# Norm roots on ScalarE, their inverses and the rotary turn on VectorE, GpSimd left with the gathers

## What is computed

```
def rms_norm(x, g):
    y = xf * rsqrt(mean(xf * xf, axis=-1) + EPS)
    return y * g

layer:
    h = modulate(rms_norm(x, norm1), shift, scale)            # 1024 wide
    z = h @ w_in                                              # q, k, v | pool | cq, ckv, krope
    q_na, k_na = rms_norm(q_na), rms_norm(k_na)               # per head of 64
    q_mla = rms_norm(rms_norm(cq) @ w_uq)                     # per head of 96
    ckv = rms_norm(ckv);  k_mla = rms_norm([ckv @ w_ukv, krope])
    sample tokens: the last 32 of each head of q_mla and k_mla get an axial rotary turn
    three mixers (windowed attention, pooling, latent attention) -> x = x + g1 * (mix @ w_out)
    h2 = modulate(rms_norm(x, norm2), shift, scale)
    experts: 8 heads x 16 experts of 16384 per token; u row . h2 -> gelu -> sum of weighted v rows
    x = x + g2 * experts
```

## Time and profile before

| | us |
|---|---|
| median of 3 runs | 4089.07 (4085.47 to 4100.49) |
| the profiled execution's own time | 4087.34 |
| its span, first to last instruction | 4084.9 |
| PE busy | 3017.2 (74%) |
| DVE busy | 2633.4 (64%) |
| POOL busy | 2578.4 (63%) |
| ACT busy | 365.9 (9%) |
| moved over the span | 1504.70 MB, 1342.34 MB of them by the gathers |

### The profile page before, as it was taken

The page is one execution under the profiler, slowest core; times in us unless marked ns, Lnnn a source line. Parts: engine busy times, 40 slices in busy tenths (PEclk is TensorE's granted clock), DMA queues, the critical chain, the costliest instruction groups (busy, mean ns, idle before and its releaser), DMA issues.

```text
span 4084.9 us, 36679 instructions
## 1 busy us (share of the span) xinstructions
PE 3017.2 (74%) x10978; PEld 1092.4 (27%) x10978; DVE 2633.4 (64%) x7013; ACT 365.9 (9%) x1055; POOL 2578.4 (63%) x2836
## 2 busy tenths in 40 slices
PE   7888988778766666777767888877777766666666
PEld 4534443223222122322211335332322301011000
DVE  2555568768665665667667555776776767666663
ACT  2112111101000010101000111110100000000000
POOL 1157357667575666766667654656776777777775
PEclk8999799878787677877866997888887967676667
DMA  7887999999999999999999997999999999999998
GB/s 280 307 299 281 325 378 406 390 396 397 360 373 389 399 366 342 348 341 409 387 408 406 332 338 264 349 373 379 398 384 354 395 409 408 404 405 403 400 409 343
DMA packets 453356, 1504.70 MB, mean 368 GB/s; under 512 B 47108, under 2 KB 67368, under 8 KB 452648
## 3 DMA queue, kind: packets, MB, share of 16 engines
q0 software_dynamic: 368640, 1342.34, 84.9%
q1 hardware_dynamic: 84108, 159.92, 10.8%
q10 hardware_dynamic: 412, 0.11, 0.0%
HBM read 1496.52 MB, written 5.67 MB: 368 GB/s over the span
## 4 chain that ended last, share of the span: by engine, by line
DMA 35%; PE 28%; POOL 19%; issue 12%; DVE 5%; ACT 1%; SPq 0%; ACTq 0%; DVEq 0%; POOLq 0%
DMA expert_rows<-in_peer_v,pair_experts 28%; POOL expert_rows L1105 18%; PE expert_sum L2267 11%; DMA expert_rows<-in_peer_u,experts 5%; PE work L1993 4%; PE work L2193 3%; PE work L2208 2%; DVE expert_rows L1903 2%; PE work L2129 2%; PE work L1939 1%; PE work L2156 1%; PE work L1968 1%; POOL stat_rstd L1055 1%; PE work L2174 1%; DMA weight_ring<-in_w_mod 1%
## 5 line engine op out<-in xcount | busy, mean ns | idle before, releaser
L2267 PE MATMUL expert_sum<-expert_rows,weight_columns 128*32 128x512 f32 x5120 | 1704.5, 767 | 849.8 <-DMA expert_rows<-in_peer_v,pair_experts 839.5
L1903 DVE CUSTOM_DVE_ANT_0 expert_rows<-expert_rows,tokens 128x1024 f32<-128x1024 f32 x1280 | 1558.8, 1218 | 865.1 <-DMA expert_rows<-in_peer_u,experts 856.3
L1105 POOL DMA_INDIRECT expert_rows<-in_peer_v,pair_experts x1280 | 1228.1, 959 | 780.1 <-PE expert_sum L2267 526.3
L1105 POOL DMA_INDIRECT expert_rows<-in_peer_u,experts x1280 | 1214.7, 949 | 475.4 <-issue 346.5
L2267 PEld LDWEIGHTS expert_sum<-expert_rows,weight_columns 128*32 128x32 f32 x5120 | 213.4, 119 | 1794.4 <-DMA expert_rows<-in_peer_v,pair_experts 1550.8
L1993 PE MATMUL work<-weight_ring,h_or_mixed 128*128 128x384 f32 (+3 forms) x768 | 258.3, 494 | 15.4 <-DMA weight_ring<-in_w_in 8.4
L1939 PE MATMUL work<-ident,scratch 128*128 128x128 f32 (+1 forms) x770 | 153.7, 327 | 119.3 <-DVE scratch L1501 41.9
L1993 PEld LDWEIGHTS work<-weight_ring,h_or_mixed 128*128 128x128 f32 x768 | 146.8, 207 | 145.2 <-issue 86.7
L2208 PE MATMUL work<-h_or_mixed,weight_ring 128*128 128x128 f32 (+1 forms) x1024 | 166.2, 320 | 8.5 <-DMA weight_ring<-in_peer_wq 3.5
L1939 PEld LDWEIGHTS work<-ident,scratch 128*128 128x128 f32 (+1 forms) x770 | 101.3, 161 | 264.6 <-issue 118.2
L2208 PEld LDWEIGHTS work<-h_or_mixed,weight_ring 128*128 128x128 f32 x1024 | 145.7, 203 | 64.5 <-issue 57.2
(11 more groups left out here) (210 smaller groups left out, 2706.2 us busy)
## 6 DMA issues: line engine op xcount, KB each, us to landing
weight_ring<-in_w_mod SPq DMA_DIRECT2D x20, 2048.0 KB, 14.7
expert_rows<-in_peer_u,experts POOLq DMA_INDIRECT x1280, 7.7
expert_rows<-in_peer_v,pair_experts POOLq DMA_INDIRECT x1280, 7.6
weight_ring<-in_w_in SPq DMA_DIRECT2D x11, 1536.0 KB, 14.9
weight_ring<-in_peer_wq SPq DMA_DIRECT2D x8, 2048.0 KB, 12.6
weight_ring<-in_w_out SPq DMA_DIRECT2D x7, 2048.0 KB, 19.1
mla_qkv_or_x_and_queries<-in_w_out SPq DMA_DIRECT2D x8, 1280.0 KB, 6.3
expert_rows<-in_w_mod SPq DMA_DIRECT2D x4, 2048.0 KB, 14.1
```

The source lines that it names most:

```text
L1105: g.indirect_dma_start(buffer, None, table, bass.IndirectOffsetOnAxis(ap=numbers[:, col:col + 1], axis=0),).then_inc(row_in, 16)
L1903: v_.tensor_tensor_reduce(out=u_ring[r % U_RING], in0=u_ring[r % U_RING], in1=tokens[:, :], scale=1.0, scalar=0.0, op0=ALU.mult, op1=ALU.a ...
L2267: ins = t_.matmul(acc[to:to + STRIP_T, hf * 512:(hf + 1) * 512], spread[:, at:at + STRIP_T], v_buffer(row)[:, hf * 512:(hf + 1) * 512], st ...
```

## The change

POOL no longer takes part in norms or in the rotary turn; after the setup its stream holds gathers alone.

- ACT's squares are scaled by n**-0.5 where the mean was wanted (`mean_scale`), so sums become means; for A and uq they stay sums, as before.
- ACT does a new step `root` right behind each of its squares: `stat_std` = Sqrt(sum + eps). For the six-head norms it waits there for DVE's sums.
- DVE does a new step `inverse` ahead of each scaling: a reciprocal of the root and one Newton step (three `scalar_tensor_tensor`), each waiting for the one before it, on 128x1 or 128x6 values.
- DVE does the rotary turn right behind the gain of the same tile, in four instructions instead of six.
- The waits on a free slot of sums now go by DVE's last step of the norm (`inverted`) instead of POOL's power.

```
@@ POOL @@
-            def rstd(key, n, mul, add):
-                pool.wait_ge(*stats.filled(key))
-                if stats.before(key):
-                    pool.wait_ge(*rows_scaled(stats.before(key)))
-                g.tensor_scalar(stat_cols(stp, key, n), stat_cols(stat, key, n), mul, add, ...)
-                pool.wait_ge(stat_biased, rstd_ready.at(key))
-                g.tensor_tensor(stat_cols(rst, key, n), stat_cols(stp, key, n), half[:, 0:n], ALU.pow)...
...
-            does = {"nx": norm, "pr": project, "up": queries_up, "kv": keys_up, "us": rope_queries,
-                    "ks": rope_keys_of, "row": expert_row}
+            does = {"row": expert_row}
@@ ACT @@
+            def root(key, n):
+                at = {"A": 1, "uq": 2}.get(key[0], 0)
+                if stats.before(key):
+                    sc.wait_ge(*inverted.done(stats.before(key)))
+                sc.wait_ge(setup, EPS_SET)
+                sc.wait_ge(*stats.filled(key))
+                a_.activation(stat_cols(std, key, n), stat_cols(stat, key, n), ACT.Sqrt,
+                              bias=eps[:, at:at + 1]).then_inc(std_ready.sem, 1)
...
-                    a_.activation(sq[:, 0:WIDTH], bank(key)[:, 0:WIDTH], ACT.Square).then_inc(squares.sem, 1)
+                    a_.activation(sq[:, 0:WIDTH], bank(key)[:, 0:WIDTH], ACT.Square,
+                                  scale=mean_scale(key)).then_inc(squares.sem, 1)
+                    root(key, HEADS)
...
@@ DVE @@
+            def inverse(key, n):
+                dve.wait_ge(*std_ready.done(key))
+                no, eps_ = inverted.at(key), EPS * {"A": DH, "uq": QK}.get(key[0], 1)
+                y, t, m = inv[:, 0:n], inv[:, 8:8 + n], stat_cols(stat, key, n)
+                v_.reciprocal(y, stat_cols(std, key, n)).then_inc(inverse_step, 1)
+                dve.wait_ge(inverse_step, 3 * no - 2)
+                v_.scalar_tensor_tensor(out=t, in0=y, scalar=-0.5, in1=y, ...)
+                dve.wait_ge(inverse_step, 3 * no - 1)
+                v_.scalar_tensor_tensor(out=t, in0=m, scalar=eps_, in1=t, ...)
+                dve.wait_ge(inverse_step, 3 * no)
+                v_.scalar_tensor_tensor(out=stat_cols(rst, key, n), in0=t, scalar=1.5, in1=y, ...)
+                dve.wait_ge(*inverted.done(key))
...
-                dve.wait_ge(*rstd_ready.done(key))
+                inverse(key, HEADS)
                 for a in range(2):
                     ins = per_head(key, q[:, 3 * a:3 * a + 3, :], ps[:, a, :, :], 3 * a, 3)
                 ins.then_inc(banks.frees(key), 1)
                 dve.wait_ge(*banks.freed(key))
                 gain_mul(key, q, G_MQ, QK)
+                rope(key)
...
+            def rope(key):
...
+                for s in range(2):
+                    v_.tensor_tensor(crossed[:, :, :, s, :], halves[:, :, :, 1 - s, :], sin..., ALU.mult)
+                v_.tensor_tensor(v, v, cos, ALU.mult).then_inc(rope_step, 1)
+                v_.tensor_tensor(v, v, turned, ALU.add).then_inc(roped.sem, 1)
```

More of the change, by code:

```diff
@@ L788, in build @@
         squares = Steps(sem("squares_ready"), [k for k in sq_turns if k[0] in ("A", "B", "uq", "ukv")])
[L789 to L790 removed]
+        inverse_step = sem("inverse_step")
+        std_ready = Steps(sem("std_ready"), stat_turns)
+        inverted = Steps(sem("std_inverted"), [
+            ("uq", *s[1:]) if s[0] == "us" else ("ukv", *s[1:]) if s[0] == "ks" else s[1:] for s in plan
+            if s[0] in ("nx", "us", "ks") or s[0] == "sc"])
         tokens_scaled = Steps(sem("tokens_scaled"), [s[1:] for s in of_kind("nx")])
@@ L1031, in _ @@
             g.memset(ident[:, :], 0.0).then_inc(setup, 1)
-            g.memset(half[:, :], -0.5).then_inc(setup, 1)
+            for i, n in enumerate((1, DH, QK)):
+                g.memset(eps[:, i:i + 1], n * EPS).then_inc(setup, 1)
             pool.wait_ge(setup, IDENT_CLEARED)
@@ L1313, in key_squares @@
                 sc.wait_ge(*assembled.done((l, b)))
-                a_.activation(sq, qn(key), ACT.Square).then_inc(squares.sem, 1)
+                a_.activation(sq, qn(key), ACT.Square, scale=mean_scale(key)).then_inc(squares.sem, 1)
+                root(key, HEADS)
             def pooled(l, grp, g):
```

93 lines of the change are left out of this document (41 added, 52 removed).

## The result

The changed kernel takes 4109.2 us (median of 20 runs, 4089.5 to 4132.0), the kernel before 4090.1 in the same series: ratio 1.0038 (95% interval 1.0023 to 1.0053), slower by 16 us by the ratio, 19 by the medians. The forecast was 4062 us, 26 us faster by its sum; 4109.2 lies within its 4008 to 4120, but on the other side of the kernel before.

The account below looks back on a forecast made before the run. Gathers bound stretches nearly without norms, PE layer 0's and the last heads, POOL's place in the plan's order layer 1's first heads. From 4087.3 us, -30 - 10 - 6 + 12 + 8 = -26 gave 4061, written 4062; range 4008 to 4120.

Parts of the forecast that it names:

- the head: Program start, no gathers: ten added table loads, six roots and inverses cost +12 us, between +4 and +24.
- the last heads: 2246 to 2433 us, bound by PE: freeing POOL gives -6 us, between -20 and +8.
- part of +8: Standing-alone norms, nine n2 and five layer 1 n1: each load delays PE's transpose 1.6 us; +8 us total, 0 to 20.
- POOL freed in layer 1's first heads: 1477 to 1838 us: gathers no longer held up by POOL's norms and turns; -30 us, between -55 and -5.
- POOL freed in layer 0's heads: 176 to 434 us, bound by PE with 44.7 us idle: -10 us, between -35 and +12.
- the new chain: Each norm: root plus four chained DVE instructions, 1.2 us without a load, 2.5 with one.
- at nothing: Dot products queued behind DVE's added work: no cost beyond 13 us already deducted, as four-row rings cover 10 us.
- rival A: Slower: ACT's stream becomes the bound, in the head and at norms between exponentials; +44 us, 4131 us, chance 0.16.
- The table load: ACT, 81 added loads: 1.28 us each, 104 us; the skill's rule with drain would make 215 us.
- Rival D: ACT's table switches cost twice the load's row, 1.28 us more on 31 loads: +40 us, 4102 us, chance 0.03.
- B: No change: PE's long products or weight-chunk bandwidth hold back the gathers' gain; +2 us, 4090 us, chance 0.24.
- C: Larger gain: all the room in the three head stretches is taken; -80 us, 4007 us, chance 0.12.

Follow-up runs that it names:

- second pair: Profiles of the kernel before and the changed kernel, both unchanged, rerun together on another chip: ratios 1.0016 and 1.0028.
- e7: Changed kernel with GpSimd made to stand at the plan's norm steps until the root is made, computing nothing there: ratio 1.0062 to the kernel before.
- e10: Changed kernel without the Newton step, so one reciprocal in place of four chained instructions per norm: ratio 0.9979 to the kernel before.
- e9: Kernel before plus four chained one-column copies (0.8 us) on VectorE ahead of every D and E norm's scaling: ratio 1.0047 to the kernel before.
- e3: Changed kernel with the rotary turns back on GpSimd, only the norms moved: ratio 1.0006 to the kernel before.
- e1: Changed kernel with Identity in place of Sqrt, so no table switch and scales not the reference's: ratio 0.9952 to the kernel before.
- e11: Changed kernel with D and E norms back on GpSimd except in layer 1's blocks 0 to 2: ratio 1.0031 to the kernel before.
- e2: Kernel before with the new path only for norms of layer 1's blocks 0 to 2 and turns of blocks 1 and 2: ratio 0.9936.
- e15: Same kernel as e2, run again on another chip: ratio 0.9922 to the kernel before.

## Why the prediction was wrong, point by point

By place, first and second pair of profiles: the head +12 forecast, +25 and +18 measured; layer 0's heads (rows 0 to 65) -10, +20 and +18; layer 1's first heads (rows 410 to 515) -30, -22 and -26.5; the last heads and what is behind them to row 858 -6 and part of +8, +22 and +24. In the second pair rows 65 to 92 gave 12 back.

**POOL freed in layer 1's first heads: right.** -30 forecast, -22 and -26.5 measured (rows 410 to 515), with the share at 0.96 to 0.97. By bandwidth it fell short (365 to 371 GB/s, not 385); PE's v waits were not halved (58.1). e7 shows that the gathers' freedom is about half of it.

**POOL freed in layer 0's heads: this is the step that failed.** -10 forecast. Rows 16 to 56 grew by 19 to 21 us (16 at the same products of PE); with what rows 56 to 92 gave back in the second pair, rows 16 to 92 are +5 to +19. PE was 81% busy in rows 0 to 65, not 86%. I had taken the new chain as 1.2 us against 1.65 for six heads and 0.8 for one column. That compared two chains as if both stood alone. The old one ran on POOL while DVE, the engine that scales, was busy with rows; its visible cost to PE was nothing at the D norm shown. The new one is some 0.8 us in DVE's own queue, and stood in full in PE's wait at four D and E norms in a row. I had written that DVE's work is "queued" ahead of the dot products, and costed it "at nothing", with 15 to 20 us in the three head stretches if that fails; but not that the norm's consumer is the same queue. e10 shows the size: three instructions less in the chain, and the ratio falls from 1.0028 to 0.9979. The second part of this loss, the longer wait for the weight chunk, was in no term; what makes the chunk late is open.

**And the price of a wait.** I priced a microsecond of PE waiting as a microsecond. In e9, 5.7 us of idle time more came with 7.1 us of longer busy time for the same products, at a granted clock of 0.92 in place of 0.96. The sum also put 2246 to 2433 us at -6 and the n2 beyond it at part of +8; rows 666 to 858 cost 22 to 24 us, with no more idle time at all, only clock. There the longer waits are not shown as the cause.

**The head: right in kind.** +12 forecast (4 to 24), +17.9 and +25.3 measured; the first-row time scatters over 193 to 203 us in the kernels with the loads and 176 to 181 in those without (185 in e9, whose D and E are late there too). The signal "later than 196 us" for rival A came in the first pair (201.5) and just missed in the second (195.7). Against e3 on the same chip e1 gives 12 us of it to the loads; the Newton step gives nothing (e10).

**The table load: the row held, not the rule.** All 83 loads last 1.28 us, in 68 of them the next activation starts within 0.05 us of the load's end, and at the other 15 it waited for DVE; ahead of a load ACT never idles 1 us. By the Trainium skill, "ScalarE: Activation LUTs", section "What ACT_TABLE_LOAD costs", each would show about 1.38 us of drain beside it; no such gap is seen. Rival D is out. A root took 0.30 us, not 0.2.

**The rivals.** The sign was A's, with a head near its +24, but not its place: loads in layer 0's heads are hidden (e1), and layer 1's first heads gained what the forecast said. B and C named the gathers, which behaved as forecast. None of the four named DVE's chain as the price. The signal I set for it, DVE over 85% busy, could not have shown it: DVE is 63 to 71% busy in the head stretches.

**Open.** Why the weight chunk asked for at row 19 lands late and is waited for at row 24 (2.5 to 7.4 us) whenever layer 0's norms are moved: not GpSimd's freedom (e7); not D and E (e9 has no such wait, e11 keeps it); and 2.5 us in e10 against 2.9 in e3 does not tell whether the chain's length has a part. And what takes the clock in rows 666 to 858.

## What to carry to other kernels

When small work moves between engines, ask first whether the engine that consumes it was ready: a slow producer beside a busy consumer can be free, and a fast chain inside the consumer's queue is not. (Where the consumer stands idle for the producer, as DVE did at half of the norms here, it is the other way.) Where TensorE runs at full clock with short waits, count what its longer waits do to the products behind, and look for it in busy time at an unchanged number of products. And move work only in the stretch whose bound it is: the same edit, confined to the rows in which the gathers waited for POOL, turned 0.3 to 0.4% slower into 0.6 to 0.8% faster (e2 and e15).
